# Delta rule on TensorE: the masked product of levels 1 to 5 as one 128-row product per chunk pair in place of two 64x64 quarters

## The reference, cut to what matters

```python
m = jnp.where(strict, jnp.einsum('bhncd,bhnsd->bhncs', k_beta, k) * decay, 0.0)
eye = jnp.eye(CHUNK, dtype=f32)
t_inv = lax.linalg.triangular_solve(eye + m, ..., lower=True, unit_diagonal=True)
u = t_inv @ v_beta
w = t_inv @ (k_beta * jnp.exp(g)[..., None])
...
v_new = u_c - w_c @ state
o = qd @ state + a_c @ v_new
state = state * gl + kd.T @ v_new
```

## Time and profile before

| | |
|---|---|
| median of 3 runs | 1491.18 us (1491.14 to 1493.94) |
| profiled execution | 1494.14 us, span of its instructions 1492.3 us |
| TensorE matmul busy | 1450.0 us, 97% of the span, 8392 records |
| weight loads busy | 1166.5 us, 78% |
| DVE, ACT, POOL busy | 577.1, 584.4 and 558.5 us (39%, 39%, 37%) |
| TensorE's granted clock, mean | 0.991 of 2.4 GHz |
| P groups (line 773) | 640 records in 40 groups, from 130.1 to 426.9 us |

### The profile page before, as it was taken

The page is one execution under the profiler, slowest core; times in us unless marked ns, Lnnn a source line. Parts: engine busy times, 40 slices in busy tenths (PEclk is TensorE's granted clock), DMA queues, the critical chain, the costliest instruction groups (busy, mean ns, idle before and its releaser), DMA issues.

```text
span 1492.3 us, 22493 instructions
## 1 busy us (share of the span) xinstructions
PE 1450.0 (97%) x8392; PEld 1166.5 (78%) x8392; DVE 577.1 (39%) x1131; ACT 584.4 (39%) x989; POOL 558.5 (37%) x270
## 2 busy tenths in 40 slices
PE   6989999999989999999999999999999999999998
PEld 5867777777767788888888887776788888888887
DVE  3556666666664322221122225674422221022210
ACT  5534454544444333322222234785433322222322
POOL 4532323223203334435443444222344444434432
PEclk9999999999989999999999999999999999999999
DMA  6422111111101233223322233111133223323232
GB/s 245 128 72 71 55 46 37 49 58 58 50 2 46 82 106 113 86 86 97 113 99 99 60 108 115 58 51 33 54 120 107 91 87 97 115 83 112 68 98 76
DMA packets 39223, 124.16 MB, mean 83 GB/s; under 512 B 4192, under 2 KB 5472, under 8 KB 39136
## 3 DMA queue, kind: packets, MB, share of 16 engines
q1 hardware_dynamic: 38976, 122.68, 25.8%
q10 hardware_dynamic: 160, 0.26, 0.1%
HBM read 120.57 MB, written 2.10 MB: 82 GB/s over the span
## 4 chain that ended last, share of the span: by engine, by line
PE 92%; DVE 4%; ACT 2%; issue 1%; DMA 0%; DVEq 0%; SPq 0%; ACTq 0%
PE bank L596 76%; PE bank L793 2%; PE bank L773 1%; ACT ws L1167 1%; PE bank L963 1%; DVE ws L1633 1%; PE bank L922 1%; DVE act_lo L1630 1%; PE bank L914 1%; PE bank L832 1%; PE bank L1123 1%; PE bank L1099 1%; PE bank L608 1%; PE bank L952 1%; PE bank L835 1%
## 5 line engine op out<-in xcount | busy, mean ns | idle before, releaser
L544 POOL TENSOR_TENSOR w_lo<-w_raw,w_hi 128x1024 fp32r<-128x1024 f32 (+1 forms) x250 | 538.0, 2168 | 780.1 <-ACT w_hi L1167 780.1
L596 PE MATMUL bank<-act_hi,w_hi 128*128 128x512 f32 (+1 forms) x1776 | 708.1, 399 | 6.7 <-DVE act_lo L1630 2.7
L596 PE MATMUL bank<-act_hi,w_lo 128*128 128x512 f32 (+1 forms) x1776 | 680.2, 383 | 0.0
L596 PE MATMUL bank<-act_lo,w_hi 128*128 128x512 f32 (+1 forms) x1776 | 679.5, 383 | 0.0
L596 PEld LDWEIGHTS bank<-act_hi,w_hi 128*128 128x128 f32 x1776 | 335.1, 189 | 77.9 <-issue 8.9
L596 PEld LDWEIGHTS bank<-act_hi,w_lo 128*128 128x128 f32 x1776 | 334.8, 188 | 65.5
L596 PEld LDWEIGHTS bank<-act_lo,w_hi 128*128 128x128 f32 x1776 | 335.5, 189 | 61.0 <-issue 4.4
L1167 ACT ACTIVATE w_hi<-w_raw 128x1024 fp32r<-128x1024 f32 (+1 forms) x250 | 230.7, 953 | 88.8 <-PE bank L596 86.6
L1624 DVE TENSOR_TENSOR ws<-bank,ws 128x512 f32<-128x512 f32 x110 | 75.8, 690 | 335.1 <-PE bank L596 325.1
L1167 ACT ACTIVATE ws<-ws 128x512 f32<-128x512 f32 (+2 forms) x128 | 82.9, 650 | 152.5 <-DVE ws L1624 111.7
L1956 DVE TENSOR_TENSOR xT<-xT,bank 128x512 f32<-128x512 f32 (+1 forms) x48 | 33.0, 687 | 257.0 <-PE bank L596 257.0
(11 more groups left out here) (170 smaller groups left out, 1032.2 us busy)
## 6 DMA issues: line engine op xcount, KB each, us to landing
w_raw<-w_stream SPq DMA_DIRECT2D x154, 512.0 KB, 3.7
w_raw<-w_out SPq DMA_DIRECT2D x32, 384.0 KB, 3.1
w_raw<-w_down SPq DMA_DIRECT2D x32, 384.0 KB, 3.1
w_raw<-w_down SPq DMA_DIRECT2D x32, 320.0 KB, 3.2
ws<-x_in SPq DMA_DIRECT2D x1, 2048.0 KB, 9.0
ws<-mem_in SPq DMA_DIRECT2D x2, 512.0 KB, 4.8
out<-ws SPq DMA_DIRECT2D x1, 1024.0 KB, 4.2
out<-ws SPq DMA_DIRECT2D x1, 768.0 KB, 3.6
```

Source lines behind the costliest of these rows:

```text
L544: nc.gpsimd.tensor_tensor(w_lo[:, s, 0:width * P], w_raw[:, s, 0:width * P], w_hi[:, s, 0:width * P].bitcast(F32), ALU.subtract).then_inc( ...
L596: mm = nc.tensor.matmul(acc, wt[:, c % RING, wsl], at[:, act0(k0 + k), off:off + n], start=(start and k == 0 and m == 0), stop=(stop and k ...
```

## The change

The P group of levels 1 to 5 becomes 4 products instead of 8. The stationary matrix is the whole 128x128 tile of `MM`, whose off-diagonal quarters are now zero, and the moving one is the packed inverse with both blocks (128 rows by 64 columns). For that, `MM` is cleared once by VectorE and afterwards holds only the two diagonal quarters of each tile. ScalarE copies them one by one, and copies the off-diagonal quarter, which level 6 needs, into the free second half of `PM`: three instructions of 64x256 in place of one of 128x512. Since `MM` must keep its zeros, the later product of line 806 is copied to `PM` instead. The semaphore `t_done` counts three per head in place of one.

```diff
@@ TensorE, delta(h) @@
                         if k == 1:
-                            pe.wait_ge(S.t_done, h + 1)
+                            pe.wait_ge(S.t_done, 3 * h + 2)
                             pe.wait_ge(S.y_done, Y_PER_HEAD * h + 1)
                         else:
                             pe.wait_ge(S.tz_done, PER_HEAD * h + tz_count(k - 1, g, last))
+                        if last:
+                            pe.wait_ge(S.t_done, 3 * h + 3)
                         for i, t in enumerate(half_tiles(g)):
                             if last:
                                 mm = nc.tensor.matmul(bank[half_rows(1), D[3 - g], HB * i:HB * (i + 1)],
-                                                      diag(MM, t, 0, 1), packed(TT, t, 0), start=True, stop=True)
+                                                      packed(PM, t, 0, 1), packed(TT, t, 0), start=True, stop=True)
                                 continue
-                            for r in range(2):
-                                mm = nc.tensor.matmul(bank[half_rows(r), D[3 - g], HB * i:HB * (i + 1)],
-                                                      diag(MM, t, r, r), packed(TT, t, r), start=True, stop=True)
+                            mm = nc.tensor.matmul(bank[:, D[3 - g], HB * i:HB * (i + 1)], tt(MM, t),
+                                                  ws[:, TT, HB * t:HB * (t + 1)], start=True, stop=True)
                         mm.then_inc(S.p_mm, 1)
...
-                        mm = nc.tensor.matmul(v_acc, tt(MM, t), state[:], start=False, stop=True)
+                        mm = nc.tensor.matmul(v_acc, tt(PM, t), state[:], start=False, stop=True)
...
-            pe.wait_ge(S.rw_cols, 6)
+            pe.wait_ge(S.rw_cols, 7)
@@ ScalarE, delta(h) @@
-                act.wait_ge(S.z_pre, 2 * h + 2)
-                a(w(MM), psum(D[1]), ACT.Copy).then_inc(S.t_done, 1)
+                for r, c in ((0, 0), (1, 1), (0, 1)):
+                    if r == c:
+                        act.wait_ge(S.z_pre, 2 * h + r + 1)
+                    rows_, from_ = half_rows(r), psum4(D[1])[half_rows(r), :, HB * c:HB * (c + 1)]
+                    to = w4(MM)[rows_, :, HB * c:HB * (c + 1)]
+                    if r != c:
+                        to = ws[rows_, PM, SEQ // 2:].rearrange("p (t c) -> p t c", t=NT)
+                    a(to, from_, ACT.Copy).then_inc(S.t_done, 1)
                 fill(0)
@@ VectorE, ahead of head 0, and delta(h) @@
             V.memset(w(ZZ), 0.0).then_inc(S.rw_cols, 1)
+            V.memset(w(MM), 0.0).then_inc(S.rw_cols, 1)
...
-                cp(w(MM), psum(D[2])).then_inc(S.nw_done, 1)
+                cp(w(PM), psum(D[2])).then_inc(S.nw_done, 1)
```

## The result

| | before | changed |
|---|---|---|
| median of 11 runs | 1492.13 us (1491.14 to 1495.21) | 1496.26 us (1494.62 to 1498.12) |
| ratio, 95% interval | | 1.0022 (1.0013 to 1.0031) |
| profiled execution, span | 1494.14, 1492.3 us | 1496.28, 1494.5 us |
| matmul records | 8392 | 8072 |

The change makes the kernel 0.22% slower, about 3.3 us, with 1.9 to 4.6 as the interval. (The two medians differ by 4.1 us.

The account below looks back on a forecast made before the run. TensorE was taken as the bound, with 92% of the chain that ended last. 2.7 (heads 0 to 6) + 0.8 (head 7) + 0.5 (clearing) = 4.0 us on 1491.2 gave 1495.2 us, range 1492.2 to 1498.2.

Parts of the forecast that it names:

- P groups of heads 0 to 6: 35 groups in TensorE's full stream, each 0.08 us longer by the nearest line; 2.7 us slower taken.
- The step of 0.11 us at 64 columns: Each of a group's 8 new records takes 0.11 us, set by the 128x128 float32 load, not the columns.
- The gap of 0.36 us: TensorE's idle "issue" time ahead of 35 groups, from turning to 64x64 quarters; 12.7 us in all, which goes.
- the span forecast at 1.35 us: Last filling product ahead of a P group to the second behind it: 1.35 us, where it was 1.27.
- P groups of head 7: Without filling work, the first half's result comes later; levels 2 to 5 pay 0.2 us each, 0.8 us slower.
- The first level: Head 7's first P group follows line 755 without a wait while VectorE is busy with another copy; nothing counted.
- The clearing: A third VectorE clearing in the chain ahead of head 0 delays the convolution TensorE waits for; 0.5 us, once.
- Counted as nothing: ScalarE's three copies, some 0.8 us more per head, the level 6 wait and the moved copy cost nothing.
- The sum: Whole kernel: 2.7 + 0.8 + 0.5 = 4.0 us slower, 1495.2 us.
- More slow clock: Rival: TensorE's clock falls already in head 7's levels, 1 to 3 us more, about 1497.3 us; 12%.
- Loads that hide: Rival: the 64-column pass sets the step in the P groups, 14.7 us less, 1478 us; 6%.
- Hardly any loss: Rival: step a little under 0.11 and better overlap, or less slow clock; 2.2 us slower, 1493.4 us; 22%.

Follow-up runs that it names:

- run 1: On the changed kernel, every 128-row product of the P group issued twice: 1532.01 us, ratio 1.0267 to the kernel before.
- run 2: On the kernel before, every 64x64 quarter product of the P group issued twice: 1508.62 us, ratio 1.0107.
- run 3: On the changed kernel, the P group's products pass 128 moving columns, the same 64 twice: 1496.25 us, ratio 1.0024 to the kernel before.
- run 4: On the changed kernel, each 64-column product of the P group split in two of 32 columns: 1538.51 us, ratio 1.0307 to the kernel before.
- run 5: On the changed kernel, an extra 64x64 product behind the first product of each half of a P group: 1533.61 us, ratio 1.0272 to the kernel before.
- run 6: On the changed kernel, 64x64 quarters in the P group again, clearing and ScalarE's three copies kept: 1491.81 us, ratio 1.0004 to the kernel before.
- run 10: On the kernel before, the P group's upper quarter product issued twice, the lower once: 1508.32 us, ratio 1.0115.
- run 8: On the changed kernel, 64x64 quarters in the P groups of head 7 alone: 1494.09 us, ratio 1.0019 to the kernel before.
- run 7: On the changed kernel, four more VectorE clearings of 128x512 behind the third: 1497.44 us, ratio 1.0041 to the kernel before.
- run 11: On the kernel before, VectorE's four small copies ahead of head 0 moved behind the first tile's convolution: 1488.34 us, ratio 0.9977.

## Why the prediction was right, step by step

**P groups of heads 0 to 6: 2.7 us forecast, 2.84 in the trace.** The step of 0.11 us at 64 columns, taken from 32 and 128 columns, measured 0.112 in run 1. The gap of 0.36 us was read as TensorE's and is one of the weight loads, but the whole turn costs 0.35 (run 2), so the size was right. The gap went, no wait took its place, and the span forecast at 1.35 us came out at 1.35 in the level shown and at 1.36 in the mean. Runs 1, 3 and 4 show that the step goes by the number of load and product pairs and not by the columns that pass; runs 2 and 5 show what stood on the other side, and run 6 that the P groups are all of the loss in these heads. That the load is what sets the step is the likely reading, and no run changes the load alone. For it speaks that a record of a 64x64 quarter, whose load has half the columns, has half the step (0.058 us, run 10).

The Trainium skill, "TensorE: Matmul & The Clock Gate", section "LDWEIGHTS (loading the stationary operand)", has the time of a load go by its columns, at columns / 1.2 ns; for 128 columns that makes, as an estimate, 107 ns. The steps of 0.112 and 0.058 us agree with it in proportion and are a little more.

**P groups of head 7: 0.8 us forecast, 0.95 measured.** The level's 1.88 us was as worked out: first mask late by 0.2, second half of little weight. Four levels give 0.8. The first level, counted at nothing since it has no wait ahead, costs 0.15 from line 755 on, and 0.12 of that is there with quarters too (run 6), with ScalarE's exponentials late by 0.3 us. The new form itself costs head 7 13.43 - 12.61 = 0.8 us, against runs 6 and 8.

**The clearing: 0.5 us forecast, 0.0 measured.** This is the step that failed. The prediction saw that the clearing stood in the chain that ended last, and took the whole step of 0.53 us as added; TensorE's wait for the convolution was to be 1.8 us and is 1.32. But the instruction behind it in that same chain, the first small copy, ended when GpSimd's subtraction did, whenever it had started itself. In the earlier trace rows the four copies of 128x32 show 2.19 us, where run 7 has 0.40; that length was the sign of the wait, and it was read as work. Run 7 shows the cover.

**Counted as nothing** (ScalarE's three copies, the wait at level 6, the copy to `PM`): right to within 0.1 us by run 6, which keeps them all.

**The sum.** 2.84 + 0.95 + 0 = 3.8 us by the traces, against 4.0; two terms were a little small and the third was too large, so that the sum is nearer than its terms, which is luck. The ratio gives 3.3 us, with 3.8 well inside its interval. The median of 1496.26 is 1.1 us over the forecast, as the median of before in these runs is 0.9 us over the one that the forecast started from.

**The rivals.** More slow clock: the changed kernel's levels ran at 2.4 GHz in its profile. With half the columns behind each of twice the loads, or with turns, head 7 did stand at 1.2 GHz (runs 4 and 5), so the clock could have decided. Loads that hide: the step would have had to be under 0.102, and it is 0.11 from 32 to 128 columns. Hardly any loss: the ratio's interval (1.9 to 4.6 us) reaches down to that case's 2.2 us; against it stands the trace, with 3.8.

## What to carry to other kernels

Before merging small products into fewer large ones, compare step times and not counts: here a float32 product with a 128x128 stationary matrix costs two records of 0.11 us whether 32 or 128 columns pass, two 64x64 quarters run side by side at 0.058 us a record each, and the turn from one form to the other and back costs 0.35 us once per group. With sixteen quarter records to a turn the two forms are nearly even (16 x 0.029 + 0.35 = 0.82 against 8 x 0.111 + 0.02 = 0.91); by the same arithmetic, an estimate that no run tests, they meet at twelve or thirteen, and with fewer the full product would win.

Where a short instruction shows a long time in the chain that ended last, ask what held it before adding its neighbours up: work put ahead of it may be free, and moving it behind the work that isn't held gained 1.5 us by the trace here (3.4 by the ratio, the rest unexplained).

## What the runs showed of the hardware that was not expected

- Two diagonal 64x64 quarters overlap in the three orders tried. 16 records on one with 8 on the other cost what 16 on each cost, 0.46 to 0.47 us more a group (runs 10 and 2), and 8 on each cost nearly the same written one side after the other (a span of 1.32 us in place of 1.27 for 8 of each, in the mean of 35 groups). The fuller quarter sets the time.
- A float32 copy of 128x32 elements on VectorE lasted 1.90 us beside a GpSimd subtraction, while clearings of 128x512 (0.48 us) and the convolution (0.75 us) beside it kept their times (runs 7 and 11).
- In head 7, which has no filling work, the granted clock was 1.00 (2.4 GHz) through the levels in run 1, and 0.50 (1.2 GHz) for 27 us in run 4, which has as many loads and half the columns behind each.
